# A hybrid decoder trunk: the order of filling projections and softmax blocks on TensorE

## The reference

```
q, k, v = split(h @ even_w_in)                 # 8 heads of 64
score   = sum_h w_h * relu(q_idx_h . k_idx)    # an indexer picks 256 keys for each query
logits  = q . k_sel / 8 + bias(q_pos - k_pos)  # per head
out     = softmax(logits) @ v_sel
mix     = concat(out * silu(ag), gla_out) @ even_w_out
```

## Time and profile before

| | us |
|---|---|
| median of 3 runs (lowest, highest) | 1007.27 (1004.72, 1009.28) |
| the profiled execution | 1007.82 |
| its span, first to last instruction | 1005.7 |
| PE busy, share of the span | 960.0, 95% |
| DVE busy | 639.4, 64% |
| ACT busy | 530.9, 53% |
| POOL busy | 343.1, 34% |
| first logits of block 0 / first matmul of the output projection, from the span's start | 381.85 / 596.07 |

### The profile page before, as it was taken

The page is one execution under the profiler, slowest core; times in us unless marked ns, Lnnn a source line. Parts: engine busy times, 40 slices in busy tenths (PEclk is TensorE's granted clock), DMA queues, the critical chain, the costliest instruction groups (busy, mean ns, idle before and its releaser), DMA issues.

```text
span 1005.7 us, 15058 instructions
## 1 busy us (share of the span) xinstructions
PE 960.0 (95%) x5650; PEld 783.8 (78%) x5650; DVE 639.4 (64%) x1100; ACT 530.9 (53%) x909; POOL 343.1 (34%) x437
## 2 busy tenths in 40 slices
PE   7969999999999999999999789999999999999997
PEld 5858798888777776767777568888888888888885
DVE  5328899669889854636464744674649393989252
ACT  6626778876765443545454763333355372775211
POOL 0012065256868453433231661110522231225200
PEclk9979999999999999999999999999999999999999
DMA  9651011101133241331010643222212111113062
GB/s 354 157 89 47 6 44 43 43 22 42 55 103 95 75 142 37 128 113 40 18 54 22 240 144 129 86 82 83 84 47 59 42 48 57 42 36 125 8 209 83
DMA packets 69982, 83.88 MB, mean 83 GB/s; under 512 B 3432, under 2 KB 52632, under 8 KB 69912
## 3 DMA queue, kind: packets, MB, share of 16 engines
q1 hardware_dynamic: 68496, 81.33, 25.2%
q10 hardware_dynamic: 1416, 1.63, 1.4%
HBM read 64.07 MB, written 18.35 MB: 82 GB/s over the span
## 4 chain that ended last, share of the span: by engine, by line
PE 56%; DVE 5%; ACT 2%; DMA 2%; issue 2%; POOL 1%; ACTq 0%; POOLq 0%; DVEq 0%
PE ps L1755 16%; PE ps L1756 15%; PE ps L1757 15%; PE ps L2026 3%; PE ps L2010 3%; PE ps L1867 1%; DMA g_two<-gla_d 1%; ACT pT L1116 1%; PE ps L1868 1%; PE ps L1869 1%; POOL g_two L783 1%; DMA gla_d<-g_two 1%; PE ps L2090 1%; DVE tmp L1624 1%; DVE prob L1523 0%
## 5 line engine op out<-in xcount | busy, mean ns | idle before, releaser
L1755 PE MATMUL ps<-hH,wH 128*128 128x512 f32 (+1 forms) x356 | 141.0, 396 | 0.9 <-DVE scaled L1505 0.9
L1756 PE MATMUL ps<-hL,wH 128*128 128x512 f32 (+1 forms) x356 | 135.6, 381 | 0.0
L1757 PE MATMUL ps<-hH,wL 128*128 128x512 f32 (+1 forms) x356 | 135.5, 381 | 0.0
L1755 PE MATMUL ps<-h1H,w_slot_H 128*128 128x512 f32 x256 | 99.8, 390 | 0.0
L1757 PE MATMUL ps<-h1H,w_slot_L 128*128 128x512 f32 x256 | 99.6, 389 | 0.0
L1756 PE MATMUL ps<-h1L,w_slot_H 128*128 128x512 f32 x256 | 99.6, 389 | 0.0
L1368 DVE TENSOR_SCALAR_CACHE_REDUCE junk<-score,cand 128x768 bf16<-128x768 f32 (+3 forms) x128 | 96.7, 811 | 1.1
L679 POOL TENSOR_TENSOR wL<-raw,wH 128x1024 fp32r<-128x1024 f32 x28 | 70.2, 2514 | 57.3 <-ACT wH L871 56.8
L676 POOL TENSOR_TENSOR w_slot_L<-raw,w_slot_H 128x1024 fp32r<-128x1024 f32 x16 | 41.3, 2585 | 125.0 <-ACT w_slot_H L867 125.0
L1755 PEld LDWEIGHTS ps<-hH,wH 128*128 128x128 f32 x356 | 67.0, 188 | 16.9 <-issue 5.2
L1755 PE MATMUL ps<-wH,hH 128*128 128x256 f32 x256 | 76.8, 300 | 3.0 <-ACT bv L957 2.3
(11 more groups left out here) (287 smaller groups left out, 2357.1 us busy)
## 6 DMA issues: line engine op xcount, KB each, us to landing
raw<-in_even_w_in SPq DMA_DIRECT2D x28, 512.0 KB, 4.0
raw<-in_odd_w_in SPq DMA_DIRECT2D x16, 512.0 KB, 3.9
xt<-in_x_cols SPq DMA_DIRECT2D x8, 512.0 KB, 8.6
xn<-in_x SPq DMA_DIRECT2D x8, 512.0 KB, 9.4
gate_d<-gst SPq DMA_DIRECT2D x16, 256.0 KB, 2.2
raw_row<-in_even_w_out SPq DMA_DIRECT2D x8, 512.0 KB, 3.3
xt<-in_x SPq DMA_DIRECT2D x8, 512.0 KB, 3.4
x_d<-xt SPq DMA_DIRECT2D x8, 512.0 KB, 2.6
```

What stands on the lines that cost most here:

```text
L1755: pe.matmul(dst, lH, rH, start=k == 0, stop=False)
L1756: pe.matmul(dst, lH, rL, start=False, stop=False)
L1757: return pe.matmul(dst, lL, rH, start=False, stop=k == nk - 1)
```

## The change

In the loop over steps, all parts of a step now stand behind the turning of the first group of block a-1, and none stands behind `weigh`. The number of parts per step and everything on the other engines stay as they are.

```diff
             groups = blocks_of[a - 1] if 1 <= a <= NW else []
             if a < NW:
                 head_logits(a)
-            for g in groups:
+            for i, g in enumerate(groups):
                 turn(g)
-                if parts:
-                    pair_part(*parts.pop(0))
+                if i == 0:
+                    while parts:
+                        pair_part(*parts.pop(0))
             if groups:
                 if pieces_at(a)[0] is not None:
                     turn_gla(pieces_at(a)[0])
```

## The result

| | before | after |
|---|---|---|
| median of 8 runs each, us | 1006.31 (1004.64 to 1009.60) | 999.90 (998.25 to 1003.99) |
| ratio of the times, 95% interval | | 0.9941 (0.9919 to 0.9964) |
| the profiled execution, us | 1007.82 | 1001.73 |
| its span, us; granted clock | 1005.7; 0.987 | 999.6; 0.988 |
| first logits to first matmul of the output projection, us | 381.85 to 596.07: 214.22 | 381.41 to 591.59: 210.18 |

The change made the kernel faster by 0.6%. The forecast was 1003.0 with a range from 1000.4, and the measured median lies 0.5 us under it. One later run of the kernel before took 5315.74 us and is left out of every figure here. In the traces the attention loop became 4.04 us shorter, where the sum said 4.25. The other 2.06 of the span's 6.1 us lie outside the loop: 0.44 ahead of it and 1.62 behind it, where both kernels issue the same instructions.

The account below looks back on a forecast made before the run. PE, busy for 95% of the span, was taken to bound the kernel. The terms -2.9 - 1.3 - 0.93 - 0.47 + 1.35 = -4.25 us, from 1007.27, gave 1003.0 us, range 1000.4 to 1006.8.

Parts of the forecast that it names:

- Point 1: Steps with parts: joining parts on PE saves 0.215 us in each of 12 steps, 2.9 us gained in all.
- Point 2: Steps 9, 17 and 25, after a product's end: waits for scaling and row sums go, 0.44 us each, 1.3 gained.
- The rival that the starts cost nothing: Steps with parts: a chain just behind PE fills the saved start gaps, so 1005.9 us; chance 0.20.
- Point 3: Pair 0 up to block 8: POOL's scaling of step 4 starts earlier and block 8's logits with it, 0.93 us gained.
- Point 4: Step 26: DVE's chain behind the last product, up to block 27's wait, comes 0.47 us earlier.
- Point 5: Steps 5, 13 and 21: the second group turns 1.38 us later; blocks 15 and 23 lose 0.79 and 0.56, together 1.35.
- The rival that this costs nothing: Steps 5, 13 and 21: the late second group's 0.79 us vanish in DVE and POOL collisions, so 1001.7 us; chance 0.20.
- The other rivals: No measurable effect, 1007.3 us, chance 0.07; longer waits slow the clock in steps 8, 16 and 24, 1019.6 us, chance 0.03.
- how the numbers follow from the sum: Whole kernel: forecast given 0.50, medians moving some 1.5 us; faster than 1002.2 us 0.28, within 0.5% 0.69, slower 0.03.

Follow-up runs that it names:

- after_later: The changed kernel with POOL's scaling of the linear attention's result in steps 5 to 8 instead of 4 to 7: median 1000.57 us, ratio 0.9937.
- between: The changed kernel, but in steps with two groups one part stands behind the first turning and the others behind the second: median 999.2 us, ratio 0.9926.
- before_again: The kernel before, unchanged, traced and timed a second time: median 1006.58 us, ratio 1.0007.
- before_third: The kernel before, unchanged, traced and timed a third time: median 1007.64 us, ratio 0.9999.
- keep_busy_before: The kernel before with 24 extra transposes of a constant on PE ahead of the output projection: median 1004.14 us, ratio 0.9979.
- all_behind: The kernel before with all parts of a step behind the weighing, none ahead of it: median 1023.75 us, ratio 1.0155.
- keep_busy: The changed kernel with 24 extra transposes of a constant on PE ahead of the output projection: median 999.75 us, ratio 0.9921.
- after_third: The changed kernel, no edit, a third trace with more runs: median 1001.33 us, ratio 0.9947.
- after_fourth: The changed kernel, no edit, a fourth trace with more runs: median 1002.05 us, ratio 0.9946.
- after_again: The changed kernel, no edit, traced and timed a second time: median 1002.01 us, ratio 0.994.

## Why the prediction was right in its sum and wrong in its number

**Point 1, the joins: right.** Step 19 shows 0.22 us. From one block's logits to the next, in the same two timelines, they came to 0.19 to 0.24 us in steps 11, 12, 18, 19 and 20, and to 0.24 to 0.28 in steps 8, 16 and 24, where 0.315 was said. Step 10 won 0.35: its first part starts 0.62 us behind the turning in before and 0.49 in after, the small wait for the weights' low half that point 2 named. The rival that the starts cost nothing (1005.9) falls: the logits of every step with parts moved by them, and no chain took them back.

**Point 2, steps 9, 17 and 25: right.** Step 9 became shorter by 0.63 us, steps 17 and 25 by 0.62, where a join and 0.44 make 0.655. Step 9 of after shows the spreading at the pace of the matmuls ahead of it:

```profile
445.48 0.39 PE L1757 MATMUL ps<-hH,wL 128*128 128x512 f32 x1
445.71 0.27 PE L2018 MATMUL ps<-ident,rl 128*128 128x128 f32 x1
445.91 0.44 PE L2026 MATMUL ps<-pT,v 128*64 128x128 f32 x4
```

0.23 and 0.20 us, where one step like it took 0.42 and 0.26.

**Point 3, pair 0: right.** POOL's scaling of step 4 started at 407.42 instead of 408.64, 1.22 us earlier, and block 8's logits 1.24 earlier. 0.44 of both lie ahead of the loop, so the term measured 0.80 against 0.93. after_later shows that this chain is what sets block 8.

**Point 4, step 26: right.** The low half of q and k, in the timelines of DVE and PE:

```profile
548.93 0.44 PE L1867 MATMUL ps<-qkH 64*128 64x384 f32 x2
...
549.95 0.69 DVE L1511 SCALAR_TENSOR_TENSOR qkL<-scaled,qkH 128x512 fp32r<-128x512 f32 x1 [0.17 <-ACT qkH L1099]
```

It starts 1.02 us behind the logits, as said, instead of 1.49, and block 27 moved by 0.48 more than block 26, where 0.47 was said.

**Point 5, the late second group: right.** In steps 21 and 22 of after:

```profile
519.22 0.45 ACT L1116 ACTIVATE pT<-ps 128x128 f32<-128x128 f32 x2 [2.21 <-PE ps L2010]
...
521.39 0.62 ACT L1099 ACTIVATE qkH<-scaled 128x512 fp32r<-128x512 f32 x1
...
522.05 0.69 DVE L1511 SCALAR_TENSOR_TENSOR qkL<-scaled,qkH 128x512 fp32r<-128x512 f32 x1 [0.65 <-ACT qkH L1099]
```

The logits of block 22 came 3.75 us earlier than before, but these three only 2.37, 2.42 and 3.01. So the copies are 1.38 us late, the split 1.33 and the low half 0.74, where 1.38, 1.38 and 0.79 were said. Block 15 lost 0.75 (0.79 said), block 23 0.51 (0.56 said). Between removes both. The rival that this costs nothing (1001.7) falls, though its number is closer to the measured median than the forecast's.

**The other rivals.** The edit has an effect in every trace. The longer waits of the steps without parts, 0.46 and 0.83 us, were not followed by a fall of the clock. The loop of after lost 0 to 3.4 us to it in four traces, that of before 1.7 to 5.1 in three.

**The step that failed: how the numbers follow from the sum.** The mechanisms of the five points held. The sum of -4.25 stands against -4.04 in the first pair of traces, -3.9 between the mean loops, and -3.7 +- 0.6 between all runs at equal clock. The step that failed is the one from this sum to 1003.0 and its range. Two things were missing in it.

First, a term: the clock. The sum put its change at nothing and gave no reason. The prediction looked for a fall only as a risk of the change. But after loses 2.8 +- 0.9 us less to the clock, worth 1.9 us by the line fitted above. The trace of before had a fall in step 27, behind waits of 1.20 us for step 26's spreading and 1.01 for block 27's logits. Point 4 shortened the first of them, and what that does to the fall behind it was not asked. All traces together give a hint. In the four with the order of before (before_again, before_third and keep_busy_before are the others) that wait is 1.20 or 1.21 us, and each loses something in steps 26 to 28: 1.7, 1.7, 5.1 and 5.1. In the nine with the order of after or between it is 0.72 or 0.73 us. Five of them lose nothing in steps 26 to 29, the others 1.7, 1.7, 3.4 and 3.4. In all_behind it is 1.20 us, and 5.1 are lost. That the shorter wait is the cause is not shown: the traces are few, and step 27 took as long with before's fall as without one. Where the 1.9 us arise stays open. The late load ahead of block 8 is a second candidate, since it came in two of those four traces and in two of seven with the new orders and POOL's scaling where it was.

Second, the scatter. The +-1.5 us was read from three runs, and the median of eight was still 1.6 us under the mean of 37. That part is the luck of a draw. The 3.1 us between 1003.0 and 999.90 are then the draw (1.6), the clock (1.9) and the reference of 1007.27, which lies 0.2 above the mean of before, less the 0.5 by which the sum was too large. The ratio said, 1003.0 / 1007.27 = 0.9958, lies inside the measured interval.

## What to carry to other kernels

Filling work between dependent steps is placed by the wait it covers, not by its amount: ahead of the spreading it hid 11 us that it does not hide behind the weighing, and in front of a later turning it delays what that turning feeds, 0.75 us here. Each join of two parts saved some 0.2 us here, so join parts where no wait is left to cover. Read the clock of every gap of a microsecond or more that the change shortens or lengthens, and put a price on the fall behind it as a term of the sum.

## What the runs showed of the hardware that was not expected

- **The clock can fall while the profile shows PE busy without a gap.** In the stretch 170 to 180 us, ahead of everything the change touches, PE was busy all the time in all traces. In 7 of 14 the clock fell and 3.4 us were lost, in one 1.7, in six nothing. Right ahead of the fall, and in it, stand matmuls whose operands fill only 16 of the 128 partitions (first row, from before: 3.9 us of them). The traces without a fall have them too, and what part they have in it was not tested. The first logits accordingly come at 381.4 to 381.9 or at 377.6 to 378.3 us (once at 379.2). The tables are of before and of keep_busy:

```profile
170.55 3.92 PE L1904 MATMUL ps<-iwblr,w 16*128 16x512 f32 x7
```

```profile
170.00:180.00 10.00, 10.00 (x36) 0.66 0.30 72
```

```profile
170.00:180.00 10.00, 10.00 (x64) 1.00 0.39 98
```

- **Waits of the same length are not followed by the same clock.** Behind waits of 1.68 to 1.88 us for block 8's logits the clock fell in between and keep_busy, and not in before, before_third, after, after_third and after_fourth. Behind 2.95 to 3.46 us it fell each time, in four traces. Behind 3.29 us ahead of the output projection it fell in ten of eleven. The Trainium skill, page "TensorE: Matmul & The Clock Gate", section "HAM oscillation — how this bites in real kernels", describes falls behind waits; the traces agree for those, and the fall at 170 us is none of them.
- **The load for POOL's scaling ahead of block 8 lands up to 1.8 us later from one execution to the next** (POOL waited 3.60 us in after and 5.32 in after_again), with no difference in the kernel. The longer wait came in four of twelve traces that have this scaling in steps 4 to 7.
